# A mixture-of-experts encoder layer: the matmul engine's expert loop is turned by half a gate product

## The reference

```python
def expert_block(args):
    tok, g, e = args
    xb = xf[tok]
    hu = xb @ w_gate_up[e] + b_gate_up[e]
    a = jnp.minimum(hu[:, :D_FF], SWIGLU_LIMIT)
    lin = jnp.clip(hu[:, D_FF:], -SWIGLU_LIMIT, SWIGLU_LIMIT)
    act = a * jax.nn.sigmoid(SWIGLU_ALPHA * a) * (lin + 1)
    return (act @ w_down[e] + b_down[e]) * g[:, None].astype(xb.dtype)
```

## Time and profile before

| | |
|---|---|
| median of 3 runs | 1294.47 us (1293.67 to 1295.86) |
| the profiled execution | 1297.64 us, of which the profile's span is 1295.9 us |
| expert loop on PE, first gate matmul to last down matmul | 319.0 to about 1265.5 us |
| PE busy | 1273.8 us, 98% of the span |
| weights read by the experts | 32 x 12 MB |

### The profile page before, as it was taken

How to read it: one execution, slowest core, us unless ns; L and a number is a source line. 1 busy time by engine, 2 the same in 40 slices (tenths; PEclk the granted TensorE clock), 3 DMA queues, 4 the chain that set the end, 5 groups by cost and what they waited for, 6 DMA issues and landing times.

```text
span 1295.9 us, 32762 instructions
## 1 busy us (share of the span) xinstructions
PE 1273.8 (98%) x13814; PEld 690.3 (53%) x13814; DVE 585.8 (45%) x984; ACT 175.2 (14%) x248; POOL 316.8 (24%) x319
## 2 busy tenths in 40 slices
PE   8999999999999999999999999999999999999997
PEld 7866778844444444455444444444444444444444
DVE  7776757564333333333333333333333334333335
ACT  4243343300000000000000000000000000000002
POOL 2135532021333332222222222222222222222210
PEclk9999999999999999999999999999999999999999
DMA  9322127589999999999999999999999999999974
GB/s 261 85 67 59 56 98 293 212 322 403 402 415 412 410 419 416 413 418 413 419 418 414 415 417 421 412 419 417 417 412 413 419 413 417 419 417 414 417 276 141
DMA packets 95374, 450.26 MB, mean 347 GB/s; under 512 B 12208, under 2 KB 37280, under 8 KB 45936
## 3 DMA queue, kind: packets, MB, share of 16 engines
q1 hardware_dynamic: 84288, 430.47, 81.5%
q0 software_dynamic: 9568, 18.97, 5.6%
q10 hardware_dynamic: 1488, 0.40, 0.1%
HBM read 439.54 MB, written 18.67 MB: 354 GB/s over the span
## 4 chain that ended last, share of the span: by engine, by line
PE 94%; DVE 2%; DMA 1%; issue 1%; ACT 1%; DVEq 0%; SPq 0%; POOLq 0%; ACTq 0%
PE gu_bank L1825 50%; PE bank L1839 24%; PE bank L1592 5%; PE bank L1594 4%; PE bank L1593 4%; PE first_gu_bank L1825 2%; PE bank L1676 1%; PE bank L1842 1%; PE bank L1690 1%; PE bank L1653 1%; PE bank L1801 1%; DMA x_sb<-in_x_dram 1%; DMA sum_rows<-y_out,scatter_list 1%; PE fin_bank L1898 0%; DVE probs_a L1188 0%
## 5 line engine op out<-in xcount | busy, mean ns | idle before, releaser
L1825 PE MATMUL gu_bank<-raw,xT 128*32 128x512 f32 x2976 | 326.4, 592 | 0.0
L1457 DVE TENSOR_TENSOR gate_in<-gu_bank,b_gu 128x768 f32<-128x768 f32 x31 | 29.7, 958 | 540.2 <-PE gu_bank L1825 540.2
L1825 PEld LDWEIGHTS gu_bank<-raw,xT 128*32 128x32 f32 x2976 | 118.7, 110 | 200.7 <-issue 196.7
L649 POOL DMA_INDIRECT x_got<-xn_rows,gather_list x96 | 114.6, 1193 | 332.7 <-DVE xT L1468 300.0
L1839 PE MATMUL bank<-raw_a,aT 128*32 128x256 f32 x2232 | 167.3, 379 | 0.0
L1825 PE MATMUL gu_bank<-raw_c,xT 128*32 128x512 f32 x1488 | 166.7, 592 | 0.0
L1842 PE MATMUL bank<-raw_a,aT 128*32 128x256 f32 x744 | 165.6, 379 | 0.0
L1839 PEld LDWEIGHTS bank<-raw_a,aT 128*32 128x32 f32 x2232 | 111.2, 110 | 57.3 <-issue 16.1
L1825 PEld LDWEIGHTS gu_bank<-raw_c,xT 128*32 128x32 f32 x1488 | 59.4, 110 | 100.4 <-issue 98.3
L935 ACT ACTIVATE sig_in<-gate_in 128x768 f32<-128x768 f32 x32 | 27.1, 846 | 631.9 <-DVE gate_in L1461 631.9
L1839 PE MATMUL bank<-raw_b,aT 128*32 128x256 f32 x1152 | 96.0, 380 | 0.1
(11 more groups left out here) (282 smaller groups left out, 1637.3 us busy)
## 6 DMA issues: line engine op xcount, KB each, us to landing
raw<-in_w_gate_up_dram SPq DMA_DIRECT2D x128, 1024.0 KB
raw_c<-in_w_gate_up_dram SPq DMA_DIRECT2D x62, 1024.0 KB
raw_a<-in_w_down_dram SPq DMA_DIRECT2D x62, 1024.0 KB
raw_b<-in_w_down_dram SPq DMA_DIRECT2D x32, 1024.0 KB
raw_e<-in_w_gate_up_dram SPq DMA_DIRECT2D x31, 1024.0 KB
raw_d<-in_w_down_dram SPq DMA_DIRECT2D x31, 1024.0 KB
raw_b<-in_w_gate_up_dram SPq DMA_DIRECT2D x30, 1024.0 KB
raw<-in_w_in_dram SPq DMA_DIRECT2D x24, 512.0 KB, 6.2
```

The costliest lines, as they stand in the source:

```text
L649: pool.indirect_dma_start(out=x_got[:, r, :], out_offset=None, in_=xn_quarters, in_offset=bass.IndirectOffsetOnAxis(ap=gather_list[:, r:r ...
L1457: dve.tensor_tensor(gate_in[:, :, :], gu[:, :, 0:QUARTER], gate_b, ALU.add)
L1825: ins = pe.matmul(gu[c * GROUP:(c + 1) * GROUP, r, :], x[:, i, r * GROUP:(r + 1) * GROUP], w[:, c], start=first, stop=last)
```

## The change

PE's loop is cut at another place. `job` becomes two functions: `head` has the waits at the top and gate chunks 1 to 4, and `rest_of_job` has gate chunks 5 to 8, the wait for the activation and the down products. Ahead of the loop now stand the whole of job 1 and the head of job 2. Then the number of bodies is read, and the loop runs once less (29 bodies here): each body is the rest of a job and the head of the next. Behind the loop stands the rest of the last job, and then the last down products as before. The order of the matmuls, their operands and the semaphores they wait for and raise are the same; the number of `head`'s job is one more computed value.

```diff
--- before.py
+++ after.py
@@ -1863,15 +1863,21 @@
                 if i == 1:
                     sum_lists()
 
-            def job(n, b=0):
-                j, turns = job_no(pe, n, b), turns_of(pe, b)
+            HEAD = GU_CHUNKS // 2
+
+            def head(n, j, turns):
                 if n == 1:
                     pe.wait_ge(lists_taken, 2)
                     pe.wait_ge(extra_ready, 1)
                 else:
                     pe.wait_ge(gu_taken, j)
                 pe.wait_ge(x_gained, j)
-                for i in range(GU_CHUNKS):
+                for i in range(HEAD):
+                    m = gu_chunk(n, i)
+                    gate_up(m, i, turns[m // RAW])
+
+            def rest_of_job(n, j, turns):
+                for i in range(HEAD, GU_CHUNKS):
                     m = gu_chunk(n, i)
                     gate_up(m, i, turns[m // RAW])
                 pe.wait_ge(aT_ready, fixed(pe, j * DN_CHUNKS))
@@ -1881,11 +1887,17 @@
                     m = dn_chunk(n - 1, i)
                     down(m, i, turns[m // RAW])
 
-            job(1)
+            assert BODY == 1
+            head(1, 1, turns_of(pe, 0))
+            rest_of_job(1, 1, turns_of(pe, 0))
+            head(FIRST, FIRST, turns_of(pe, 0))
             count = bodies(pe)
-            with pe.Fori(0, count) as b:
-                for n in range(FIRST, FIRST + BODY):
-                    job(n, b)
+            whole = pe.snap(count - 1)
+            with pe.Fori(0, whole) as b:
+                j, turns = job_no(pe, FIRST, b), turns_of(pe, b)
+                rest_of_job(FIRST, j, turns)
+                head(FIRST + 1, fixed(pe, j + 1), turns)
+            rest_of_job(FIRST, job_no(pe, FIRST, whole), turns_of(pe, whole))
             turns = turns_of(pe, count)
             for i in range(DN_CHUNKS):
                 m = last_dn_chunk(i)
```

## The result

| | before | changed |
|---|---|---|
| median of 4 runs | 1294.07 us (1293.29 to 1295.86) | 1282.76 us (1282.23 to 1284.83) |
| ratio, 95% interval | | 0.9919 (0.9906 to 0.9932) |
| the profiled execution's span | 1295.9 us | 1280.5 us |
| expert loop: first gate matmul of job 2 to the first matmul of the last two down products | 319.01 to 1255.13 = 936.1 us | 316.98 to 1242.34 = 925.4 us |

The changed kernel is 11.3 us faster. The forecast was 1283.6 us, with a range of 1276.5 to 1290.

What follows compares the result with a forecast made beforehand. PE's chain of bodies was taken to bound the kernel, with the DMA engines full too. Seams gave 10.9 us, the gate chain and loads 0, taking the median from 1294.47 to 1283.6 us, range 1276.5 to 1290.

Steps and rivals of the forecast that it cites:

- The chain leaves the seam: Between last down and first gate matmul: the sequencer's 0.8 us branch chain moves away, 0.42 us less at usual seams.
- The sum: Time above 0.16 us from last down to first gate matmul, over all 30 seams: 10.9 us.
- The chain is hidden in the gate: Between gate chunks: the 0.8 us chain fits under a 1.9 us sequencer lead; cost 0, at most 6 us.
- The hold stays: Among the last down matmuls: the sequencer's delay of about 1.3 us remains, showing 0.24 us a body.
- rival B: The hold before the seam goes with the branch: 6.2 us more gained, about 1277 us; chance 0.15.
- The hint of the earlier trace: POOL's third gather starts 1.3 us before the usual seam's chain; before the short seam POOL has nothing for 7.5 us.
- The loads: SP's loads in the loop: PE won't wait for them; priced at 0.
- the spare time: Loads in the ring: issued 29 us before use, landing some 8.5 us after issue, leaving 20 us.
- D: Full DMA engines hold PE back in the loop, so no gain: 1294 us; chance 0.06.
- C: A longer hold, or 0.2 us a body at the new place, returns half the gain: about 1289 us; chance 0.09.
- E: The loop's jump back fetches instructions, 1.0 us at each of 28 back edges: slower, about 1311 us; chance 0.08.
- The tail: Behind the loop: same work, 11 us earlier; the clock drop may shift, 1.5 us allowed either way.

Runs made afterwards that it cites:

- chip Q: Group timed on one chip: kernel before 1282.70 us; changed kernel 1282.00, kernel before with gathers late 1282.85, changed kernel cut behind gate chunk 8 1282.14.
- chips P: Group on one chip: kernel before 1282.85 us; gathers late 1284.07, in changed kernel 1283.10; eight more sequencer steps 1297.08 in before, 1281.62 in changed.
- S: Group timed on one chip: kernel before 1292.39 us; kernel before with gathers late 1281.94, the same with lighter loads 1276.89.
- chip R: Group timed on one chip: kernel before 1292.62 us; with gathers late and lighter loads 1275.63, changed kernel with lighter loads 1283.54.

## Why the prediction was right, and where its steps were not

**The chain leaves the seam: right.** The usual seam is 0.18 us and the gate's first load follows the two remaining steps at once. The sum named 10.9 us, of which 10.3 in the stretch of the loop; that stretch became 10.8 us shorter. Where the half microsecond more comes from was not found.

**The chain is hidden in the gate: right.** The step before the branch comes 2.1 us ahead of the load behind it (1.9 was forecast), the branch 2.0 us, the steps end 1.5 us before that load, and no gap shows. Eight steps more did not show either.

**The hold stays: right, and what it hangs on is now shown.** The usual period is 31.2 and not 31.0 us. Over the loop it still costs the changed kernel 925.4 - 918.4 = 7.0 us against PE's own pace, about what rival B priced (6.2 us). It did not go with the branch. It went, in all jobs of every trace, when the gathers were moved, and with them moved the branch at the seam was free. The hint of the earlier trace rows was right, and the 1.3 us named there is the distance that the held steps keep from the third gather.

**That the hold is the same everywhere: a premise that failed.** The forecast took the count of held seams from one execution and allowed three seams more or fewer. On chip Q nearly all seams of the kernel before are free, on chips P and Q it takes 1282.7 to 1282.9 us, and on Q the change is worth 0.1%. The forecast held because the result was measured where the holds were long, as in the profile that it was read from. That much of it was luck. From the one profile this could not be told; what it could have said is that the gain hangs on a hold of 1.3 us meeting a lead of 1.1.

**The loads: no wait, as forecast, but the spare time was mis-sized.** A landing of 8.5 us was read from the point where half of the DMA engines had run dry. But PE waits for the slowest. The row of 1254 to 1256 us of the kernel before still has a DMA share of 0.24, and the next two 0.09 and 0.06. The last load was issued at 1245.09 and its last packet ended at 1260.05, so it needed 15.0 us and not 8.5:

```profile
1254.00:1256.00 2.00, 2.00 (x33) 0.95 (x25) 0.47 (x1) 0.00 (x0) 0.00 (x0) 1.00 0.24 100
```

Counted by packets in order (128 of 8 KB a load), the spare time was about 21 us late in the loop of before and 12.4 in the changed kernel's. In the late-gathers kernel on chip Q PE began to wait when this count still gave 9 to 10 us. So some 10 of the 20 us were never there, and the change used most of the rest. The sentence "if the spare time were gone, every further microsecond of gain would be lost" is what chips P, Q and S show: D was wrong for this measurement, and its mechanism is what stops the next gain. Rival B's 1277.4 could not have come even if the hold had gone; with whole loads it gave 1281.9.

**C: not seen.** No gap at chunk 5, and holds of about the same size.

**E: not seen.** 24 packets of instructions for 29 bodies, none of them in the steady loop. The Trainium skill, "Runtime: NRT & Kernel Launch", section "Instruction fetch mechanics", has a fetch behind every taken branch that leaves the current window; at neither place of the cut does a trace of this case show one.

**The tail: within its allowance for the median.** In the profiled execution it gave 2.6 us, more than the 1.5 allowed; with the 1.0 us ahead of the experts, it is why the span fell by 15.4 us, while the forecast for a profiled execution was 10.9.

## What to carry to other kernels

Put a loop's branch and its register steps behind wide matmuls, where the sequencer was 2 us ahead here, and not behind narrow ones, where it was 1.1. It cost nothing in any run, and it was worth 11 us where the sequencer was held for long. Before a gain is booked, measure the next resource by its slowest part: the load that lands last, not the mean of the queues. And look for what holds the sequencer, since exchanging two calls on GpSimd gave about the same as turning the loop. A gain of 1% should be seen on more than one chip.

## What the runs showed of the hardware

- Indirect gathers issued by POOL go with holds of PE's sequencer, which waits for nothing of theirs at that place. Where it was held, PE's next step came mostly 0.3 to 0.6 us or 0.9 to 1.6 us late (it is due 9.09 us behind the first down matmul), and with the gathers elsewhere it was on time in every job. Held steps kept 1.25 to 1.40 or 0.5 to 0.7 us from the start of the third gather. How the one reaches the other was not tried, nor was the third gather moved alone.
- How often the hold is the long one differs by group: 26 or 27 jobs in the traces of the first measurement and of chip R, 2 to 7 in those of P and Q. Of five groups two had a kernel before of 1283 us and three one of 1292 to 1294, with no overlap in any run. Whether this belongs to the chip or to something that was placed differently there stays open.
- A compare-and-branch of PE's that jumps back took 207 to 213 ns in every trace, wherever it stood, but for one in each of 240 to 253 ns; the last, which does not jump, took 76.
- The loads, at 415 to 418 GB/s with a DMA share of 1.0, are slower than they look from the mean: where PE waits on them, a body takes 31.8 us, while PE alone needs 30.96. With 1/24 less to load, the wait is gone. The last load landed 15.0 us after its issue, while the mean DMA share was down to 0.44 between 1252 and 1254 us, 6 to 8 us before that.
